# Product keys, two chained products and gathered expert rows: one block in place of four, ScalarE for half of the one-hot rows, v loaded two rows at a time

## What is computed

```
q  = (hf @ w_q).reshape(T, 8, 2, 128)                 # 8 heads, two halves
sc = einsum('thpd,hpkd->thpk', q, subkeys)            # 128 keys for each half
s1, i1 = top_k(sc[:, :, 0], 16); s2, i2 = top_k(sc[:, :, 1], 16)
cand = s1[..., :, None] + s2[..., None, :]            # 256 candidates a head
top_s, pos = top_k(cand, 16)                          # 16 of them
idx = 128 * i1 + i2 at pos; gate = softmax(top_s)     # 128 experts a token, of 16384
act = gelu(sum_d u[idx] * h); out = sum_k gate * act * v[idx]
```

## Time and profile before

| | |
|---|---|
| runs, us | 3451.11, 3452.93, 3649.39 (median 3452.93) |
| profiled execution: span | 3467.7 us |
| mean granted TensorE clock | 0.928 |
| PE, DVE, ACT, POOL busy in the span | 88%, 50%, 31%, 14% |
| DMA | 624.04 MB, mean 180 GB/s |

### The profile page before, as it was taken

The page is one execution under the profiler, slowest core; times in us unless marked ns, Lnnn a source line. Parts: engine busy times, 40 slices in busy tenths (PEclk is TensorE's granted clock), DMA queues, the critical chain, the costliest instruction groups (busy, mean ns, idle before and its releaser), DMA issues. The chain is left out here.

```text
span 3467.7 us, 33649 instructions
## 1 busy us (share of the span) xinstructions
PE 3066.9 (88%) x12681; PEld 2229.5 (64%) x12681; DVE 1723.3 (50%) x3505; ACT 1076.1 (31%) x1596; POOL 488.8 (14%) x357
## 2 busy tenths in 40 slices
PE   7887999699999598778979879698898986999998
PEld 3445666444444244564746568698898986888887
DVE  2255422200000205543442328787879797788886
ACT  2133421100000126674421222234434443333332
POOL 0000000111111000000000000003314143344442
PEclk9995999699999798889779989899999998999999
DMA  3110061488888210021002211357859688999996
GB/s 142 44 50 25 1 145 64 194 329 309 313 315 309 85 49 37 25 97 44 1 26 102 83 55 61 123 193 246 324 178 336 233 305 292 342 369 374 368 374 238
DMA packets 159776, 624.04 MB, mean 180 GB/s; under 512 B 12161, under 2 KB 84481, under 8 KB 128257
## 3 DMA queue, kind: packets, MB, share of 16 engines
q1 hardware_dynamic: 90496, 319.87, 26.1%
q0 software_dynamic: 50688, 276.85, 21.1%
q10 hardware_dynamic: 18432, 25.17, 2.0%
HBM read 555.76 MB, written 66.09 MB: 179 GB/s over the span
## 5 line engine op out<-in xcount | busy, mean ns | idle before, releaser
L1841 POOL DMA_INDIRECT RG<-in_un,EI x128 | 181.6, 1419 | 1400.0 <-DVE EI L2060 1105.3
L2275 PE MATMUL bank<-VH,GL 128*128 128x512 f32 x768 | 300.2, 391 | 29.9 <-DVE VR0r L2264 29.9
L2277 PE MATMUL bank<-VH,GH 128*128 128x512 f32 x768 | 299.7, 390 | 0.0
L1841 POOL DMA_INDIRECT RG<-in_vn,EI x128 | 216.5, 1691 | 446.7 <-DVE X L1855 429.9
L1133 PE MATMUL bank<-UP,HX 128*128 128x512 f32 x480 | 213.0, 597 | 9.4 <-DVE HX L1087 5.5
L1194 DVE SCALAR_TENSOR_TENSOR HN<-SLU,HR,bank 128x256 f32<-128x256 f32 x44 | 21.1, 481 | 344.2 <-ACT SLU L1168 344.2
L2275 PEld LDWEIGHTS bank<-VH,GL 128*128 128x128 f32 x768 | 144.8, 189 | 60.7 <-issue 30.4
L1855 DVE SCALAR_TENSOR_TENSOR X<-RG,DG,X 128x1024 f32<-128x1024 f32 x128 | 164.1, 1282 | 28.2 <-DMA RG<-in_vn,EI 24.1
L1825 PE MATMUL bank<-HTl,UH1r 128*128 128x384 f32 x512 | 174.5, 341 | 0.0
L1826 PE MATMUL bank<-HTh,UH1r 128*128 128x384 f32 x512 | 174.2, 340 | 0.0
L1825 PE MATMUL bank<-HTl,UH0r 128*128 128x384 f32 x512 | 173.3, 338 | 0.0
(11 more groups left out here) (518 smaller groups left out, 6569.3 us busy)
## 6 DMA issues: line engine op xcount, KB each, us to landing
UR<-in_u SPq DMA_DIRECT2D x64, 1024.0 KB, 5.5
VR<-in_vn SPq DMA_DIRECT2D x32, 2048.0 KB, 9.2
W<-in_weights SPq DMA_DIRECT2D x20, 1536.0 KB, 7.3
W<-in_weights SPq DMA_DIRECT2D x14, 2048.0 KB, 8.2
aspill<-GA ACTq DMA_DIRECT2D x128, 192.0 KB, 2.0
wspill<-VR SPq DMA_DIRECT2D x12, 2048.0 KB, 9.2
WW<-wspill SPq DMA_DIRECT2D x32, 768.0 KB, 13.9
AV<-aspill SPq DMA_DIRECT2D x32, 768.0 KB, 16.0
```

The source lines that it names most:

```text
L1841: e.indirect_dma_start(RG[q % RR], None, d["un" if what == "u" else "vn"][:, :], off).then_inc(*row_in[q % RR].up(16))
L2275: e.matmul(bk, r(gl[:, a, t]), r(vh[:, a, :]), start=g == 0 and a == 0, stop=False)
L2277: i = e.matmul(bk, r(gh[:, a, t]), r(vh[:, a, :]), start=False, stop=g == 31 and a == 3)
```

## The change

All four blocks become one. Buffers that live at different times share memory by explicit offsets (`vault`, `desk`) instead of by nesting. What moves or changes in each queue:

- SP issues the gains for the gathered block, the first three query loads and the first three loads of u at the start of the block.
- ACT and DVE split the first query weights ahead of, and between, the copies that make HTh and HTl. DVE splits the first two loads of u inside the searches. The first products can begin behind the last scores; product 0 and 1 wait only for the query copies out of the two PSUM banks.
- A choosing step has 0.95 first products in place of 1.2, eight are left for behind the last outer step (`BRIDGE`), and none beside the second ones (`BESIDE` is 0). So the four choosing parts have 13, 14, 13 and 14, and each outer part 22.
- Two of the four rows of OB are made on ACT: |iota - index|, and then relu(gate - gate * that), with a wait of ACT for itself in between. `pe_outer` waits for both engines. The copy IN holds the negated indices and gates.
- The second search of a choice works in place, without the buffer C2.
- The second stage loads A and v per step: v two rows of 1024 (1 MB), A 384 KB, into three buffers each. The high parts VH and GH have two buffers, the low parts are written over the loaded tile. W is still loaded per two steps. A step covers both halves of the columns, and `act_v(n)` waits for step n-2 (VH had three buffers before).
- Block 3 of the output is written early, the others as they are done.

```diff
-                shares = [1.2 if step < 14 or (step - 14) % 47 < 14 else 0.0 for step in range(NM)]
-                rest = (128 - sum(shares)) / (NM - 56)
+            BRIDGE, BESIDE, ROWS1 = 8, 0, 120
+            shares = [0.95 if x else 0.0 for x in choosing]
+            rest = (128 - BRIDGE - BESIDE - sum(shares)) / (NM - 56)
...
+            def act_hot(e, n):
+                if n % 32 == 0:
+                    e.wait_ge(*c_ia(n // 32 + 1))
+                if n >= 2:
+                    e.wait_ge(*o_mm(n - 1))
+                for j in (2, 3):
+                    t = 4 * n + j
+                    k = as_(e.activation(AB[n % 2][:, j - 2, :], cc("iota"), ACT.Abs, bias=IN[:, 0, t:t + 1]))
+                e.wait_ge(as_.sem, k)
+                for j in (2, 3):
+                    t = 4 * n + j
+                    i = e.activation(OB[n % 2][:, j, :], AB[n % 2][:, j - 2, :], ACT.Relu, bias=IA[:, 2, t:t + 1], scale=IN[:, 1, t:t + 1])
+                i.then_inc(*h_act.up(1))
...
+            def load_a(e, n):
+                for q in (2 * n, 2 * n + 1):
+                    e.wait_ge(*ga_done[q % 4](16 * (q // 4) + 16))
+                if n >= 3:
+                    e.wait_ge(*y_mm(n - 2))
+                e.dma_start(AV[n % 3][0], AD[n // 2][:, 2 * (n % 2):2 * (n % 2) + 2, :]).then_inc(*a_in[n % 3].up(16))
+            def load_v(e, n):
+                if n >= 3:
+                    e.wait_ge(*y_mm(n - 2))
+                e.dma_start(VR[n % 3][0], d["vn"].rearrange("(p g a) n -> g p a n", p=128, g=64)[n]).then_inc(*v_in[n % 3].up(16))
...
+                @block.sync
...
+                    for n in range(2):
+                        e.wait_ge(*ws_done[n](16 * NC // 2))
+                    e.wait_ge(*o_mm(96))
+                    for n in range(64):
+                        if n % 2 == 0:
+                            load_w(e, n // 2)
+                        load_a(e, n)
+                        load_v(e, n)
+                        if n >= 2:
+                            for q in beside(n - 3):
+                                if q % 2 == 0 and q // 2 + 3 < 64:
+                                    load_u(e, q // 2 + 3)
...
+                @block.scalar
...
+                    for step in range(NM):
+                        for q in firsts(step):
+                            if q % 2 == 0 and q >= 2 and q // 2 + 1 < 64:
+                                act_u(e, q // 2 + 1)
+                            act_first(e, q)
+                        choice, h, o = matrix(step)
+                        if choice:
+                            act_chosen(e, *choice)
+                        if h is not None:
+                            act_hot(e, h)
+                        if o is not None:
+                            act_outer(e, o)
...
+                @block.vector
...
+                    for n in range(64):
+                        if n < 63:
+                            dve_v(e, n + 1)
+                            if n < 62:
+                                dve_prod(e, n + 2)
+                            dve_gate(e, n + 1)
...
+                        for q in later(n):
+                            dve_row(e, q)
```

More of the change, by code:

```diff
@@ L1785, in program @@
             RR = 4
[L1786 to L1790, removed]
+            RGA = sb("RG", [128, RR, 1024], c0)
+            RG = [RGA[:, n, :] for n in range(RR)]
+            HH_, HL_ = (sb(n, [128, 8, 512], c0) for n in ("HTh", "HTl"))
@@ new lines, in pe_scores @@
+            def pe_scores(e, h):
+                e.wait_ge(*p_qt(2 * h + 2))
+                e.wait_ge(*qs_in[h % 3](16 * (h // 3) + 16))
+                for tb in range(4):
+                    n = 4 * h + tb
+                    if n >= 4:
+                        e.wait_ge(*p_sk(n - 3))
+                    for p in range(2):
+                        i = e.matmul(bank[2 + n % 4][:, span(p)], QT[h % 2][:, p, span(tb)], QS[h % 3][:, span(p)], start=True, stop=True)
+                    i.then_inc(*p_sc.up(1))
@@ new lines, in act_chosen @@
+            def act_chosen(e, tb, part):
+                if part == 12:
+                    e.wait_ge(*c_off(CHOSEN.index(tb) + 1))
+                    e.activation(PF[:, 1], PF[:, 0], ACT.Exp).then_inc(*c_exp.up(1))
+                if part == 13 and tb < 3:
+                    e.wait_ge(*c_flip(tb + 1))
+                    flipped = bank[5][:, 0:384].rearrange("p (a t) -> p a t", a=3)
+                    e.activation(IN[:, :, span(tb)], flipped[:, 1:3], ACT.Copy, scale=-1.0)
+                    e.activation(IA[:, :, span(tb)], flipped, ACT.Copy).then_inc(*c_ia.up(1))
@@ new lines, in pe_outer, with act_outer @@
+            def pe_outer(e, n):
+                e.wait_ge(*h_hot(n + 1))
+                e.wait_ge(*h_act(n + 1))
+                if n >= 3:
+                    e.wait_ge(*o_copy(n - 2))
+                for j in range(4):
+                    i = e.matmul(bank[2 + n % 3][:, span(j)], OA[n % 2][:, j, :], OB[n % 2][:, j, :], start=True, stop=True)
+                i.then_inc(*o_mm.up(1))
+            def act_outer(e, n):
+                c, t0 = 4 * n // TW, (4 * n) % TW
+                e.wait_ge(*o_mm(n + 1))
+                if t0 == 0 and c >= 2:
+                    e.wait_ge(*ws_done[c % 2](16 * (c // 2)))
+                e.activation(WS[c % 2][:, :, t0:t0 + 4].rearrange("p i t -> p t i"), bank[2 + n % 3].rearrange("p (t i) -> p t i", t=4), ACT.Copy).then_inc(*o_copy.up(1))
@@ new lines, in beside @@
+            def beside(n):
+                if n < 0:
+                    return range(NA, NA + BRIDGE)
+                done = lambda m: NA + BRIDGE + min(BESIDE, (m * BESIDE) // 40)
+                return range(done(n), done(n + 1))
+            turns = np.cumsum([0.0 if x else ROWS1 / (NM - 56) for x in choosing])
+            rows = lambda step: range(0 if step == 0 else round(turns[step - 1]), round(turns[step]))
+            later = lambda n: range(ROWS1 + n * (256 - ROWS1) // 61, min(256, ROWS1 + (n + 1) * (256 - ROWS1) // 61))
```

816 lines of the change are left out of this document (390 added, 426 removed).

## The result

The changed kernel takes 3480.58 us (median of 20 runs) against 3464.91 for the kernel before, measured beside it: 1.0051 times as long, 95% interval 1.003 to 1.0073. That is 18 us slower by the ratio and 16 by the medians, where 22 us faster was forecast; both lie within 2%. Ratios are taken over executions in the faster of the chip's two states, while the trace of the experiment "DVE's rows ahead of u's low part" is of one in the slower (3495.8 us).

The account below looks back on a forecast made before the run. PE bounds the choosing parts and second stage, whose loads just keep up; DVE is fullest in the outer parts. Terms -22 - 40 + 25 + 19 - 4 = -22 us, so 3452.9 becomes 3431; range 3350 to 3495.

Parts of the forecast that it names:

- Start: Before the choice: query loads no longer wait for the norm block, searches start 14 us earlier; 22 us saved, bounds 15 to 26.
- Choosing parts: The four parts that choose, with fewer first products on PE: 110 + 57 + 59 = 226 us in all.
- Outer parts: Three parts with outer products: PE waits 1.4 us for ACT's OB rows in 11 steps; 144 us each, 432 against 409.5.
- The bound of 160: Upper bound in us for one outer part, if coupled as badly as the first one today; the lower was 127.
- Bridge: Behind the last outer product: u(63) lands late behind nine loads, second stage starts at T + 54, not T + 29; +25 us.
- Second stage: The last 64 steps: same matmuls, bytes and DVE work, but lost buffer slack costs 0.3 us a step; +19 us.
- Tail: Kernel's end: last DMA a quarter of the 2 MB, two additions behind the last matmul instead of three; -4 us.
- rival 1: Outer parts: ScalarE's rows are hidden, PE doesn't wait, each part 129 us; -45 more, 3386 us; chance 0.20.
- rival 2: Second stage keeps 8.2 us a step and u(63) arrives in time; -19 - 12, 3400 us; chance 0.16.
- Rival 4: Second stage paced by its loads, 9.4 us a step in place of 8.5; +61, 3492 us; chance 0.12.
- Rival 5: Outer parts: Abs not in gelu's table, each of 66 gelus brings two table loads; +169, 3600 us; chance 0.03.

## Why the prediction was wrong

It forecast a gain of 22 us, and there is a loss of 18 in the runs and of 22.7 between the profiles (-16.3 - 10.8 + 28.8 + 25.6 - 4.6, in the order of the points below, the second and third together: 227.4 + 459.4 for 697.6). Point by point:

- **Start, -22 us: -16.** The searches started 12.8 us earlier (14 forecast), but they and the splits among them took 4 us more than forecast.
- **Choosing parts, 226 us: 227.4** (54.0, 58.4, 58.9, 56.1). Right.
- **Outer parts, "I take 144 for each": 163.7, 141.8 and 153.9, in all 459 for 432.** This is the step that failed, by 27 of the 45 us between the forecast and the profiles. The stall that the forecast described was there and its size nearly right (1.4 us forecast): ACT's four activations take 1.5 to 1.6 us (0.69 and 0.88 for two each) and PE waits 1.75 us, 11 times, in the middle part. What the step did not follow is the second effect of ACT's load. Only the order of ACT's queue was read. u's high part on ACT came later, DVE's low part of u waited for it, and DVE's one-hot rows waited behind. In the first and third part this made waits of 2.77 us with a lower clock behind them. With DVE's order mended the parts last 141, 143 and 142 us, so 144 holds for the stall alone. The bound of 160 was named, "coupled as badly as the first one today"; the first part exceeded it.
- **Bridge, +25 us: +29.** u 63 landed too late as worked out: 14.4 us of wait (14 forecast), 8.0 us of hand-over (8), the second stage 58 us behind T (54). The 4 us are products 126 and 127, which took 10.7 us for the 7 allowed, at a clock of 0.78.
- **Second stage, +19 us: +26, for another reason, so the nearness of the two numbers is luck.** "Matmuls, bytes and DVE work are the same" failed: the matmuls themselves were 3% slower by the placing of their operands, 15 us. The waits were 9.3 us, not 19 (0.7 before). But the 0.3 us a step that was put on the lost buffer is what showed once the pitch was restored: 19.9 us of waits over 64 steps, gone with a fourth buffer.
- **Tail, -4 us: -5.**

The rivals: rival 1 (ACT's rows hidden) is out by the waits of 1.75 us, rival 2's early u 63 by the one of 14.4. Rival 4, a second stage paced by its loads, did not come true, because the slow matmuls hid it; with the fast pitch it cost 20 us and some clock, not 61. Rival 5 is out: ACT's rows brought no table load, ten lie in the changed part of either kernel. The page of the Trainium skill (ScalarE: Activation LUTs, What ACT_TABLE_LOAD costs), by which the four rows were estimated at 1.55 us, agrees with the 1.57 of these rows. Its rule against such work on ScalarE (Rules for kernel authors) points the right way for the order as it was (1.0051 against 0.9992 with the rows on DVE), though the price came for the most part through a neighbour's queue and not through ACT's own time, and with the order mended the intervals show none (0.9787 and 0.9766).

## What to carry to other kernels

Work added to an engine is paid for by whoever is queued behind the instruction that waits for it: follow each of its products one engine further, and put what needs nothing ahead of what waits. After memory is laid out anew, read the pitch of the matmuls from their starts before any wait is explained, since a slower matmul shows in no wait and can hide a missing buffer; an edit that restores one may show nothing until the other is mended too.

## What was not expected of the hardware

A 512-column matmul of this kernel takes 0.2267 to 0.2274 us a time when its stationary and its streamed operand leave the same remainder modulo 256 as partition addresses (96 and 96, 0 and 0), and 0.2324 to 0.2334 when they don't (0 and 96, 224 and 96, 96 and 224, 0 and 224, and V's 96 against A's 224 in the kernel before). The clock was full in both. Over the 2304 matmuls of the second stage that is 13 to 15 us. That it is 256, and not another power of two, rests on two pairs: 224 against 96 is slow, which differ by 128; and with both areas at 96 the key weights lie at byte 150368 and HTh at 70240, which are 313 times 256 apart, an odd number, and are fast. Differences of less than 32 bytes weren't tried, and why it is so stays open. The 384-column first products, whose operands agree in every kernel here, had 0.1733 us throughout.
